# Attention of a decoder layer: probabilities scaled before they are turned, values held still, results in two halves of the array

## The reference, cut to what matters

```python
s = einsum('...qhgd,...khd->...hgqk', q, k) * (HEAD_DIM_ATT ** -0.5)
s = where(valid, s + bias, -inf)
m = maximum(s.max(axis=-1, keepdims=True), sink)
p = exp(s - m)
p = p / (p.sum(axis=-1, keepdims=True) + exp(sink - m))
o = einsum('...hgqk,...khd->...qhgd', p, v)
...
a = rmsnorm(att, g_att)      # over all 512 attention columns of a token
mix = concatenate([a, hm], axis=-1)
x = x + einsum('btc,cd->btd', mix, w_out)
```

## Time and profile before

| | |
|---|---|
| median of 3 runs | 2344.44 us |
| the profiled execution's own time | 2344.03 us |
| its span in the trace | 2342.2 us |
| PE busy | 2301.6 us, 98% |
| DVE busy | 1664.7 us, 71% |
| ACT busy | 1103.9 us, 47% |
| attention stretch of a quarter (scores(0) to the first `op_step`) | 75.20 us |

### The profile page before, as it was taken

The page is one execution under the profiler, slowest core; times in us unless marked ns, Lnnn a source line. Parts: engine busy times, 40 slices in busy tenths (PEclk is TensorE's granted clock), DMA queues, the critical chain, the costliest instruction groups (busy, mean ns, idle before and its releaser), DMA issues.

```text
span 2342.2 us, 37363 instructions
## 1 busy us (share of the span) xinstructions
PE 2301.6 (98%) x14430; PEld 2042.8 (87%) x14430; DVE 1664.7 (71%) x3597; ACT 1103.9 (47%) x2110; POOL 93.9 (4%) x161
## 2 busy tenths in 40 slices
PE   9999999999999999999999999999999999999998
PEld 8987899888897898898998788999878878989886
DVE  4478877776377977777456887777756788776775
ACT  4445644545345645455333564444534445444433
POOL 2000000000000000000000220000110000000000
PEclk9999999999999999999999999999999999999999
DMA  6212333234511232334521232333444112222222
GB/s 196 82 46 80 95 104 100 92 107 144 175 56 53 74 99 93 106 100 145 159 81 37 59 101 93 109 99 101 160 122 135 46 51 82 91 90 83 90 82 77
DMA packets 176652, 227.93 MB, mean 97 GB/s; under 512 B 15507, under 2 KB 126708, under 8 KB 176460
## 3 DMA queue, kind: packets, MB, share of 16 engines
q1 hardware_dynamic: 162636, 192.63, 26.4%
q10 hardware_dynamic: 6448, 19.40, 2.2%
q0 software_dynamic: 7392, 13.52, 2.1%
HBM read 214.13 MB, written 12.60 MB: 97 GB/s over the span
## 4 chain that ended last, share of the span: by engine, by line
PE 90%; DVE 7%; ACT 2%; issue 1%; DVEq 0%; ACTq 0%
PE ps L2473 18%; PE ps L2475 18%; PE ps L2474 18%; PE ps L2991 8%; PE ps L2992 8%; PE ps L2990 8%; PE ps L2484 2%; PE ps L2618 2%; PE ps L2598 1%; DVE a_lo L1457 1%; PE ps L2607 1%; DVE w_lo L1418 1%; PE ps L2664 1%; PE ps L2667 1%; DVE w_lo L1430 1%
## 5 line engine op out<-in xcount | busy, mean ns | idle before, releaser
L2473 PE MATMUL ps<-w_hi,u_all 128*128 128x512 f32 x1024 | 403.1, 394 | 1.5 <-DVE w_lo L1418 1.5
L2475 PE MATMUL ps<-w_hi,u_all 128*128 128x512 f32 x1024 | 404.2, 395 | 0.0
L2474 PE MATMUL ps<-w_lo,u_all 128*128 128x512 f32 x1024 | 400.2, 391 | 0.0
L1457 DVE TENSOR_TENSOR x<-x,ps 128x512 f32<-128x512 f32 (+1 forms) x288 | 196.0, 683 | 136.1 <-PE ps L2475 118.4
L866 ACT ACTIVATE w_hi<-PT 128x512 fp32r<-128x512 f32 x224 | 128.7, 620 | 340.9 <-PE ps L2475 237.3
L2473 PE MATMUL ps<-w_hi,a_hi 128*128 128x290 f32 (+1 forms) x768 | 262.0, 341 | 1.3 <-DVE x L1457 0.9
L2991 PE MATMUL ps<-a_lo,w_hi 128*128 128x256 f32 (+1 forms) x896 | 255.8, 285 | 0.0
L2992 PE MATMUL ps<-a_hi,w_lo 128*128 128x256 f32 (+1 forms) x896 | 255.2, 285 | 0.0
L2990 PE MATMUL ps<-a_hi,w_hi 128*128 128x256 f32 (+1 forms) x896 | 255.2, 285 | 0.0
L2474 PE MATMUL ps<-w_lo,a_hi 128*128 128x290 f32 (+1 forms) x768 | 252.6, 329 | 0.0
L2475 PE MATMUL ps<-w_hi,a_lo 128*128 128x290 f32 (+1 forms) x768 | 252.5, 329 | 0.0
(11 more groups left out here) (427 smaller groups left out, 4906.9 us busy)
## 6 DMA issues: line engine op xcount, KB each, us to landing
w_raw<-in_w_up_dram SPq DMA_DIRECT2D x128, 512.0 KB, 3.8
w_raw<-in_w_down_dram SPq DMA_DIRECT2D x128, 512.0 KB, 3.5
w_raw<-in_w_out_dram SPq DMA_DIRECT2D x32, 512.0 KB, 3.5
w_raw<-in_w_in_dram SPq DMA_DIRECT2D x24, 580.0 KB, 4.9
w_raw<-in_w_in_dram SPq DMA_DIRECT2D x22, 512.0 KB, 3.8
w_raw<-in_w_in_dram SPq DMA_DIRECT2D x32, 256.0 KB, 3.1
x<-in_x_prompt_dram ACTq DMA_DIRECT2D x9, 512.0 KB, 5.6
bias<-bias_rows POOLq DMA_DIRECT2D x32, 128.0 KB, 3.5
```

Source lines behind the costliest of these rows:

```text
L1457: return eng.tensor_tensor(out, a, b, op)
L2473: eng.matmul(out, lh, rh, start=(k == ks[0]), stop=False)
L2474: eng.matmul(out, lh, rl, start=False, stop=False)
L2475: ins = eng.matmul(out, ll, rh, start=False, stop=(k == last))
```

## The change

- DVE now scales the probabilities instead of the results. ACT's exponential also sums each head's row (`accum_out`), and `exp(sink)` is taken group by group. `invert_sums(j, g)` on DVE adds the sink's share, inverts, and multiplies the group's four heads in `wide` (128 x 1024) in place; it stands twice in each block, between the two pieces of `tm_split`. `turn_probs` waits for it (signal `p_scaled`) and not for the exponentials.
- `values(j)` holds 64 columns of `vv` still and moves 256 columns of turned probabilities: heads 0 and 2 of a group into partitions 0 to 63, heads 1 and 3 into 64 to 127 of one bank. The heads are turned in that order (`turned_slot`). The results come out as `zT` wants them, so `turn_values` and `divide` go. The bank alternates between 7 and 6.
- The squares' sums change sides: ACT squares `zT`, DVE adds four rows (`sum_squares`, a reduction from 512 to 128), and PE sums over partitions once a quarter (`value_sums`, 4 products with one moving column), after `relate(0)`. `numerators(0)` waits until DVE has read them.
- In the last block both first steps stand ahead of `turn_probs(3)`, and `low_values`, which DVE did there, come after the blocks.

```diff
 PE
             def turn_probs(q, j):
...
-                    eng.wait_ge(exp_ok.sem, exp_ok.at(q, H * j + GQ * (g + 1)))
+                    eng.wait_ge(p_scaled.sem, p_scaled.at(q, 2 * j + g + 1))
...
                 for g in range(KVH):
-                    for h in range(GQ):
-                        for half in range(2):
-                            ins = eng.matmul(values_at(g)[:, h, :], PT[:, 2 * g + half, h * P:(h + 1) * P], vv[:, j + half, g, :], start=(half == 0), stop=(half == 1))
+                    for half in range(2):
+                        for par in range(2):
+                            ins = eng.matmul(values_bank(j)[par * DH:(par + 1) * DH, 2 * g * P:2 * (g + 1) * P], vv[:, j + half, g, 0:DH], PT[:, 2 * g + half, 2 * par * P:2 * (par + 1) * P], start=(half == 0), stop=(half == 1))
                     ins.then_inc(o_out.sem, 1)
...
+            def value_sums(q):
+
+                eng.wait_ge(o_sum.sem, o_sum.at(q, BLK))
+                for j in range(BLK):
+                    ins = eng.matmul(mean_at()[:, j:j + 1], o_sums[:, j * P:(j + 1) * P], ones[:, 0:1].bitcast(F32), start=True, stop=True)
...
 DVE
+            def invert_sums(q, j, g):
...
+                eng.wait_ge(exp_ok.sem, exp_ok.at(q, H * j + GQ * (g + 1)))
+                eng.wait_ge(es_ok.sem, es_ok.at(q, 2 * j + g + 1))
+                tt(den, den, sink_share(j)[:, c], ALU.add).then_inc(den_ok.sem, 1)
...
+                eng.reciprocal(den, den).then_inc(den_ok.sem, 1)
...
+                own = wide[:, c, :] if q or j else wide[:, c, P:2 * P]
+                tt(own, own, den.unsqueeze(2).broadcast_to(list(own.shape)), ALU.mult).then_inc(p_scaled.sem, 1)
+
+            def sum_squares(q, j):
+
+                eng.wait_ge(o_sq.sem, o_sq.at(q, j + 1))
+                eng.tensor_reduce(o_sums[:, j * P:(j + 1) * P], osq.rearrange("p (i t) -> p t i", i=4), AX_X, ALU.add).then_inc(o_sum.sem, 1)
...
                 for j in range(BLK):
+                    if j:
+                        take_values(q, j - 1)
                     tm_step(o)
-                    if j == BLK - 1:
-                        divide(q, j - 1)
-                    else:
-                        tm_step(o + 1)
+                    tm_step(o + 1)
...
-                    tm_split(o - 3, 3)
+                    for k in range(2):
+                        tm_split(o - 3, 3, (k,))
+                        if j + 1 < BLK:
+                            invert_sums(q, j + 1, k)
                     if j == 1:
                         running_max(q)
...
 ACT
-                        exp(own, own, bias=st[:, 64 + h:65 + h]).then_inc(exp_ok.sem, 1)
...
+                        exp(own, own, bias=st[:, 64 + h:65 + h], accum_out=st[:, 88 + h:89 + h]).then_inc(exp_ok.sem, 1)
```

More of the change, by code:

```diff
@@ L1898, in score_max @@
                         eng.scalar_tensor_tensor(st[:, 64:72][:, c], st[:, 124:132][:, c], -1.0, nsink[:, c], ALU.mult, ALU.min).then_inc(negmax.sem, 1)
[L1899 to L1919, removed]
@@ L2101, in quarter @@
                 log_forget(q, P, slice(0, NTI), l_one, lf_ok)
+                invert_sums(q, 0, 0)
+                invert_sums(q, 0, 1)
                 def low_values(j):
@@ L2125, in quarter @@
                     if j:
-                        take_values(q, j - 1)
+                        sum_squares(q, j - 1)
                     else:
@@ L2129, in quarter @@
                             block_max(q, i)
[L2130 to L2135, removed]
                     tm_step(o + 2)
@@ L2146, in quarter @@
                     tm_step(o)
[L2147 to L2150, removed]
+                for j in range(BLK - 1):
                     low_values(j)
+                sum_squares(q, BLK - 1)
+                low_values(BLK - 1)
                 relate(q, 0)
                 weigh(q, 0)
+                eng.wait_ge(o_mean.sem, o_mean.at(q, 1))
+                eng.tensor_scalar(st[:, 96:96 + BLK], mean_at(), 1.0 / (H * DH), EPS, ALU.mult, ALU.add).then_inc(var.sem, 1)
                 eng.wait_ge(var.sem, var.at(q, 1))
@@ L2661, in numerators @@
                     eng.wait_ge(h_ok.sem, h_ok.at(q, j))
+                else:
+                    eng.wait_ge(var.sem, var.at(q, 1))
                 for i in range(2):
@@ L2883, in quarter @@
                     tm_step(o)
-                    if j < BLK - 1:
-                        tm_step(o + 1)
+                    tm_step(o + 1)
                     if j == 0:
@@ L2892, in quarter @@
                     turn_probs(q, j)
-                    if j:
-                        turn_values(q, j - 1)
-                    if j == BLK - 1:
-                        tm_step(o + 1)
-                    else:
-                        tm_step(o + 2)
+                    tm_step(o + 2)
+                    if j + 1 < BLK:
                         scores(q, j + 1)
@@ L2902, in quarter @@
                     values(q, j)
-                    if j == BLK - 1:
-                        tm_step(o + 2)
                     o += 3
-                turn_values(q, BLK - 1)
                 eng.wait_ge(r_rows.sem, r_rows.at(q, 1))
@@ L2915, in quarter @@
                 relate(q, NT, 0)
+                value_sums(q)
                 o, plan = 0, o_plan(last)
```

63 lines of the change are left out of this document (36 added, 27 removed).

## The result

| | before | after |
|---|---|---|
| median | 2344.3 us | 2352.1 us (2350.6 to 2355.6, 5 runs) |
| ratio, 95% interval | | 1.0039, 1.0027 to 1.0050 |
| span of the profiled execution | 2342.2 us | 2353.8 us |
| mean granted clock of PE in it | 0.996 | 0.985 |

The account below looks back on a forecast made before the run. PE, busy 98% of the span, was taken to bound the kernel. From 2344.0 us, PE's savings less its new waits took 9.9 and half-clock stretches added 5.6: 2339.7 us, range 2329 to 2349.

Parts of the forecast that it names:

- What PE saves: On PE, each quarter: shorter `values` 6.8 us and no `turn_values` 2.4, less 0.95 for `value_sums`; 33 us over the run.
- The rival in which the halves don't overlap: In `values`, the two 64-column halves run one after another, 3.7 us instead of 1.9; 2361 us, chance 0.06.
- The forecast waits: PE waits each quarter: 4.4 us behind `turn_probs(2)`, 0.9 more than before at `relate(0)`, 0.75 more at `value_sums`.
- For most blocks this hides: DVE's added work in blocks other than block 1: second group scaled at 10.6 us, PE wants it at 11.3; no wait.
- The clock: PE's clock after the four 4.4 us waits: one half-speed stretch of 1.4 us each, 5.6 us, bounds 0 and 11.
- The rival of late groups: At the turning, the second scaled group comes late in every block, three blocks waiting 0.8 us; 2350 us, chance 0.04.
- waits for the scalings in every block: A sign that the forecast is wrong: PE waits for the scaled probabilities in all blocks; no size given.
- the rival of the dearer clock: PE's clock costs two half-speed stretches a wait, or falls again at the blocks' end around `relate(0)`; 2346 us, chance 0.15.

Follow-up runs that it names:

- experiment 8: The changed kernel with weights' splits first, running maximum early, squares' sums behind the projection's first product, and columns ahead of the last square: 2327.0 us.
- experiments 2 and 3: The changed kernel with the running maximum behind block 0's sum of squares, alone (2335.0 us) and with the weights' split ahead of the scalings too (2331.5 us).
- experiment 1: The changed kernel with both pieces of each weights' split ahead of the two scalings again: 2342.8 us.
- 9: The changed kernel with 36 idle turnings of the identity on PE in each quarter's 4.2 us wait in block 2: 2343.5 us.
- 10: The changed kernel with idle turnings on PE in four waits of each quarter (36, 15, 10 and 6): 2338.9 us.
- 11: The kernel of experiment 8 with six idle turnings ahead of block 2's turned probabilities and nine ahead of the first numerators: 2325.0 us.

## Why the prediction was wrong

Two steps failed: the count of half-clock stretches, which made the forecast miss, and a wait that was put at nothing. The rest held.

**What PE saves** was right. The last column of the table falls from 2313.8 to 2281.5, 32.3 us (30 to 33 for a price of 0.33 to 0.40), where 33 were worked out; the halves of the array run beside each other (1.88 us, 1.9 forecast), `turn_values` is gone, and `value_sums` takes 0.81 us where the clock is whole (703.02 to 703.83 in experiment 8; 0.95 forecast). The rival in which the halves don't overlap is out.

**The forecast waits** were right in mechanism and nearly in size: 4.2 us for 4.4, at the place, with the releaser and with `running_max` in it, and experiments 2 and 3 show that its place makes it. At `relate(0)` 1.19 for 1.55, at `value_sums` 0.46 to 0.68 for 0.75 (whose own terms give 0.66), and 1.57 in the third quarter.

**A wait was overlooked.** The step that failed here is the one for the other blocks, "For most blocks this hides". There I counted when the scaled probabilities are ready, and not what the scalings push back: the second piece of the weights' split, which in block 1 PE needs at its second step, not at the turning. The prediction's own terms give it: the piece is done 4.9 + 1.28 + 1.58 + 1.28 = 9.0 us after the start of `scores`, PE is there after 1.93 + 1.9 + 3.3 = 7.1, so it waits an estimated 1.9 us; measured are 1.83 in three quarters. That is 5.8 us over the run, and 4.7 of them go when the order is undone (experiment 1). By luck the sum of the waits hid this: 4 x (4.4 + 0.9 + 0.75) - 1.1 = 23.1 us more were forecast, 24.4 came (48.9 - 24.5), mostly because those at the blocks' end grew less than forecast.

**The clock** is the term that decided: its mechanism was right and it was mis-sized, at 4 x 1.4 = 5.6 us, one stretch behind each forecast wait. In the profiled execution 51.2 us more at half clock cost 0.38 x 51.2 = 19.5 us; so -32.3 + 24.4 + 19.5 = +11.6 us, the difference of the spans. (The last column is defined by the other two, so this sum shares the difference out and does not prove the shares. The check on them is that kernels with the same work on PE agree in that column; 9, 10 and 11, less 0.109 us for each of their 144, 268 and 60 turnings, come to 2282.7, 2283.0 and 2284.4, beside 2281.1 to 2285.4 for the others with the new work. That execution is 3.5 us above the median; its clock is 0.985, the median run's 0.988. By the filled waits the term is 13 to 16 us.) Of the 12.4 us between forecast and median an estimated 10.4 are the clock (19.5 - 3.5 - 5.6, if the 3.5 us are clock), 1.3 the waits and 0.7 what PE saves. The price of one stretch was right, 3.4 x 0.38 = 1.3 us. Their number was not: four more were forecast, eight as the bound; 15 more came in the profiled execution (51.2 / 3.4): eight behind the long waits, seven at the blocks' ends and two in block 1, while two of the three in the kernel before are gone. The rival of late groups lies nearer by its number, 2350 us, but its sign, waits for the scalings in every block, is not there: PE waits for them once, 0.3 us in the third quarter. By its mechanism the rival of the dearer clock, 2346 us at 0.15, came nearest; it lacked the stretches of the overlooked wait, and it took "two stretches" and "again at the blocks' end" as one or the other, where both came.

That idle time brings the half clock is shown: the same kernel with the same late DVE and a busy PE has no half clock at the filled waits (9 and 10). The Trainium skill's page "TensorE: Matmul & The Clock Gate", section "HAM oscillation — how this bites in real kernels", has idle gaps between bursts put the clock back, and the runs agree; here single waits of 1.8 us did so in two of three quarters, and the pairs at the blocks' end (1.1 to 1.2 us, then 0.5 to 1.6) in all four. By its price, half of the time at half clock, the 51.2 us would have cost an estimated 25.6; measured are 19.5. What decides whether a given wait is followed by no, one or two stretches stays open: equal waits in one execution had all three.

## What to carry to other kernels

Work added to an engine that is off the critical path is paid for by whatever stands behind it there: go through its list instruction by instruction, the splits of weights included, and ask of each who needs its result first, not only of the results that the change is about. Where DVE's work can be put into a place where it idles, do that before giving up on a change: the same change was 0.4% slower in one order and 0.6% faster in another.

A new idle spell of TensorE can cost more than its length where PE sets the pace. In this kernel the waits of the change cost 24 us and the half clock behind them 13 to 20 more; idle turnings inside the waits, 67 in each quarter, gave 13 us of that back.

## What the runs showed of the hardware that was not expected

- Doing useless work made the kernel faster: 268 turnings of the identity took 2352.1 us down to 2338.9.
- The clock makes equal kernels scatter: the five runs of the changed kernel lie between 2350.6 us (mean clock 0.988) and 2355.6 (0.985), with the same instructions. Four equal waits of 3.7 us in one execution were followed by 0, 3.4, 3.4 and 6.8 us at half clock.
- A us at half clock cost 0.38 us here (0.33 to 0.40 by the pair of kernels compared), and that one number, taken from two kernels with PE's new work, brought the three with its old work to within 1 us of each other (2313.0 to 2314.0).
